# Rotation in four pieces one step apart, and the last unit's value products two ticks behind, in a two-layer decoder trunk on one core

## The reference

```python
def rope(t, positions):
    ...
    t1, t2 = tf[..., :half], tf[..., half:]
    return jnp.concatenate([t1 * cos - t2 * sin, t2 * cos + t1 * sin], axis=-1)

qb_rot = rope(qb, positions)                 # B: queries, 4 tiles
k_sel  = rope(ksb, positions)                # B: selected keys, 1 tile
k_win  = rope(kwb, positions)                # B: window keys, 1 tile
qc = rope(qc, positions)                     # C: queries, 4 tiles
kc = rope(kc, positions)                     # C: keys, 4 tiles
...
    w = prob[:, :, 0] - lam * prob[:, :, 1]              # differential attention
    return jnp.einsum('bhqk,bkhe->bqhe', w, v)
out = rmsnorm(out, subln_g) * (1.0 - lam_init)           # needs all of a head's output
```

## Time and profile before

| | |
|---|---|
| median of 3 runs (lowest to highest) | 1534.54 us (1533.0 to 1534.96) |
| the profiled execution | 1534.6 us |
| its span, first to last instruction | 1532.8 us |
| granted TensorE clock, mean | 0.996 |
| PE busy | 1498.8 us (98%), 7957 matmuls |
| DVE busy | 935.4 us (61%) |
| ACT busy | 634.6 us (41%) |
| POOL busy | 74.4 us (5%) |

### The profile page before, as it was taken

The page is one execution under the profiler, slowest core; times in us unless marked ns, Lnnn a source line. Parts: engine busy times, 40 slices in busy tenths (PEclk is TensorE's granted clock), DMA queues, the critical chain, the costliest instruction groups (busy, mean ns, idle before and its releaser), DMA issues.

```text
span 1532.8 us, 22548 instructions
## 1 busy us (share of the span) xinstructions
PE 1498.8 (98%) x7957; PEld 1205.8 (79%) x7957; DVE 935.4 (61%) x2197; ACT 634.6 (41%) x1499; POOL 74.4 (5%) x80
## 2 busy tenths in 40 slices
PE   8999999999999999999999999999999999999997
PEld 6778777777787777888787887777887887778885
DVE  6866755555556766454576667655555666755544
ACT  6544433334344444343444334334333444434343
POOL 1000000000000010000100000000000000000011
PEclk9999999999999999999999999999999999999998
DMA  7333332222223332332342334222222233233221
GB/s 197 84 83 90 97 77 63 56 69 62 70 63 96 93 80 83 105 105 70 107 108 69 103 83 117 56 57 62 63 63 76 70 96 89 72 101 100 86 86 72
DMA packets 250301, 129.50 MB, mean 84 GB/s; under 512 B 45690, under 2 KB 245972, under 8 KB 250196
## 3 DMA queue, kind: packets, MB, share of 16 engines
q1 hardware_dynamic: 250196, 128.13, 31.4%
HBM read 118.67 MB, written 2.10 MB: 79 GB/s over the span
## 4 chain that ended last, share of the span: by engine, by line
PE 88%; DVE 6%; ACT 3%; issue 2%; DMA 0%; SPq 0%; ACTq 0%; DVEq 0%
PE D L748 24%; PE D L750 22%; PE D L749 22%; PE Ob L936 7%; PE S L895 5%; PE T L914 4%; DVE w_lo L1304 2%; ACT w_hi L1066 1%; PE Mb L952 1%; ACT probs L1182 1%; DVE v_b L1399 1%; PE Mb L862 1%; PE Ob L940 1%; PE Mb L829 1%; DMA acc<-in_x_dram 0%
## 5 line engine op out<-in xcount | busy, mean ns | idle before, releaser
L748 PE MATMUL D<-h_hi,w_hi 128*128 128x512 f32 x1264 | 544.8, 431 | 4.7 <-DVE w_lo L1304 2.3
L750 PE MATMUL D<-h_lo,w_hi 128*128 128x512 f32 x1264 | 496.4, 393 | 0.0
L749 PE MATMUL D<-h_hi,w_lo 128*128 128x512 f32 x1264 | 494.6, 391 | 0.0
L1304 DVE TENSOR_TENSOR w_lo<-raw,w_hi 128x512 fp32r<-128x512 f32 (+2 forms) x504 | 293.9, 622 | 296.3 <-ACT w_hi L1066 296.1
L1066 ACT ACTIVATE w_hi<-raw 128x512 fp32r<-128x512 f32 (+2 forms) x504 | 263.5, 568 | 292.0 <-PE D L750 289.3
L1182 ACT ACTIVATE probs<-probs,nmax 128x128 f32<-128x128 f32 (+3 forms) x256 | 141.9, 555 | 358.7 <-DVE nmax L1554 358.6
L748 PEld LDWEIGHTS D<-h_hi,w_hi 128*128 128x128 f32 x1264 | 238.5, 189 | 65.4 <-issue 20.6
L750 PEld LDWEIGHTS D<-h_lo,w_hi 128*128 128x128 f32 x1264 | 237.3, 188 | 53.2
L749 PEld LDWEIGHTS D<-h_hi,w_lo 128*128 128x128 f32 x1264 | 239.4, 189 | 30.3 <-issue 0.5
L1554 DVE CUSTOM_DVE_ANT_0 probs<-S,maskb 128x128 f32<-128x128 f32 (+3 forms) x256 | 115.0, 486 | 44.6 <-PE S L895 28.7
L546 DVE COPY pT<-T 128x128 f32<-128x128 f32 (+3 forms) x160 | 77.4, 486 | 60.7 <-PE T L914 59.9
(11 more groups left out here) (245 smaller groups left out, 1495.6 us busy)
## 6 DMA issues: line engine op xcount, KB each, us to landing
raw<-in_w_in_dram SPq DMA_DIRECT2D x124, 512.0 KB, 3.9
raw<-in_w_in_dram SPq DMA_DIRECT2D x32, 256.0 KB, 3.8
raw<-in_w_out_dram SPq DMA_DIRECT2D x16, 512.0 KB, 4.1
raw<-in_w_ple_gate_dram SPq DMA_DIRECT2D x16, 512.0 KB, 4.2
rs<-rx SPq DMA_DIRECT2D x80, 64.0 KB, 2.0
raw<-in_cmp_w_k_dram SPq DMA_DIRECT2D x8, 512.0 KB, 3.7
raw<-in_cmp_w_v_dram SPq DMA_DIRECT2D x8, 512.0 KB, 3.8
raw<-in_w_br_a_dram SPq DMA_DIRECT2D x16, 256.0 KB, 2.9
```

The costliest lines, as they stand in the source:

```text
L748: pe.matmul(o, w_hi[:, sl, cs], hi[:, k, :], start=(k == 0), stop=False)
L749: pe.matmul(o, w_lo[:, sl, cs], hi[:, k, :], start=False, stop=False)
L750: ins = pe.matmul(o, w_hi[:, sl, cs], lo[:, k, :], start=False, stop=last)
L1304: TT(w_lo[:, sl, half], raw[:, ring(L, t, RAW), half], f(w_hi[:, sl, half]), ALU.subtract).then_inc(M["dve_lo"], 1)
```

## The change

The rotation becomes four items. "swap" (now 7 steps behind the tile's end instead of 8) holds POOL's sine product and also DVE's cosine product, which leaves the tile's end; "rot" (10 instead of 11) holds only DVE's addition; "high" (11) ACT's rounding; "low" (12) DVE's subtraction. In the last unit, V comes two ticks behind T instead of one, and Y of that unit two ticks behind the last V instead of three.

```diff
             if kind in ROTATED:
-                follow.append([8, ("swap", t)])
-                follow.append([11, ("rot", t)])
+                follow.append([7, ("swap", t)])
+                follow.append([10, ("rot", t)])
+                follow.append([11, ("high", t)])
+                follow.append([12, ("low", t)])
...
-                    vq.append((tick + 1, ti))
+                    vq.append((tick + (2 if u == UNITS - 1 else 1), ti))
...
-                            late.append((tick + (2 if u < UNITS - 1 else 3), ("Y", u)))
+                            late.append((tick + 2, ("Y", u)))
...
-        elif it[0] == "rot":
+        elif it[0] == "low":
             qk_ready.add(tiles[it[1]][:2])
...
-                        elif what == "rot":
+                        elif what == "high":
...
-                            elif kind in ROTATED:
-                                r = rots.after(t)
-                                dve.wait_ge(M["act_evac"], act_evac.after(t))
-                                if r > 1:
-                                    dve.wait_ge(M["qk_s"], r - 1)
-                                TT(rc[:], (qf if kind == "qb" else rx)[:], cosT[:], ALU.mult).then_inc(M["dve_rm"], 1)
...
                         elif what == "rot":
                             t = it[1]
-                            hi_, lo_, u = rot_dst(*tiles[t][:2])
                             r = rots.after(t)
                             dve.wait_ge(M["pool_rot"], r)
                             dve.wait_ge(M["dve_rm"], r)
                             TT(rc[:], rc[:], rb[:], ALU.add).then_inc(M["dve_rs"], 1)
+                        elif what == "swap":
+                            t = it[1]
+                            r = rots.after(t)
+                            dve.wait_ge(M["act_evac"], act_evac.after(t))
+                            if r > 1:
+                                dve.wait_ge(M["qk_s"], r - 1)
+                            TT(rc[:], (qf if tiles[t][0] == "qb" else rx)[:], cosT[:], ALU.mult).then_inc(M["dve_rm"], 1)
+                        elif what == "low":
+                            t = it[1]
+                            hi_, lo_, u = rot_dst(*tiles[t][:2])
+                            r = rots.after(t)
                             dve.wait_ge(M["act_rot"], r)
                             TT(lo_, rc[:], f(hi_), ALU.subtract).then_inc(M["qk_s"], 1)
```

## The result

The changed kernel takes 1536.39 us (median of 22 runs, 1535.73 to 1539.02), the kernel before 1534.83 us (median of 22 runs, 1532.54 to 1535.54). The ratio is 1.0016, with a 95% interval of 1.0009 to 1.0023: slower by 0.16%, some 2.4 us by the ratio (the two medians are 1.56 us apart). The profiled execution's span is 1534.4 us.

A forecast was written before the change was run, and what follows sets the result against it. PE was taken as the bound, busy 1498.8 of 1532.8 us. Losses 1.76 + 0.32 less gain 0.63 gave +1.45 a layer, +2.9 us on 1534.6: 1537.4, said as 1537.2; own range 1536.3 to 1538.3, overall 1533.0 to 1538.9.

The forecast's parts named there:

- the rival in which the chain to Y is no bound: Last unit: N of block 3 comes as soon as PE is done, gain 1.38 a layer, 1536.0 us; chance 0.13.
- Sum ahead of the maxima: At `qb1`, `qb2`, `qc0`: row maxima and PE's value products come later, loss 0.60 + 0.56 + 0.60 = 1.76 us a layer.
- Other rotations at no cost: `qb0`, `qb3`, `ksb` and C's other rotations: DVE idle over a microsecond, no cost, or 0.6 each without that cover.
- Cosine product at "swap", loss 0.32 at `kwb`: At `kwb`: POOL's sine product holds up DVE's cosine product, maxima 1.4 us late, PE 0.32 us later a layer.
- the case without the disturbance: At `kwb`, POOL not holding up the cosine product: sum and `zs` come earlier than before, gain 0.22 us.
- The last unit, gain 0.63: PE's stop for `pT` goes, 1.33 us earlier at Y, but a new 0.70 wait for `y_q`: gain 0.63 a layer.
- VectorE's waiting for ACT at the low part "gone": DVE's 19.8 us of waiting for ACT between sum and low part would be gone, without gain for PE.
- the maxima come later but PE doesn't: Value products behind the delayed maxima: PE not delayed, only the last unit counts, 1533.3 or 1533.9 us; chance 0.15.
- The faster rival: PE's stops at 180.70 and 190.21 (`kwb`) go too, up to 3.5 us a layer, 1527.5 us; chance 0.12.
- the clearly slower one: New stop at Y as long as the old, or POOL's disturbance at several of 14 rotations: 1538.8 to 1540; chance 0.15.

The follow-up runs named there:

- the last block alone: The kernel before with V two ticks behind T only for the very last block of unit 11, and Y two behind it: 1530.97 us, ratio 0.9978.

## Why the prediction was right, and where it was not

The time, the sign and the size came out: 1537.2 was said, 1536.39 measured; the working had +2.9 us, the steps in the table add up to 2.0. The time alone would have proved little. It lies 0.1 us above the lower end of my own range (1536.3 to 1538.3) and nearer to the 1536.0 of the rival in which the chain to Y is no bound. It is the trace that separates the two.

- **Sum ahead of the maxima: right in size, not quite in the path.** Said 0.60, 0.56, 0.60 a layer; measured 0.49 to 0.61, six times. Putting the sum back behind the maxima removes all six. What I had not worked out is that PE pays a part of it already at the transposes, and at `qc0` all of it: the value products there don't move away from the dense step ahead of them, because PE waited for the copy before the change too. Nor was the 0.06 us between copy and value product slack. In the changed kernel, where PE waits, the value product at `qb1` starts 0.05 us behind the copy's end as well.
- **Other rotations at no cost: right but for one.** `ksb` in layer 1 loses 0.13, since the cosine product was moved; at the others nothing over 0.1 is seen.
- **Cosine product at "swap", loss 0.32 at `kwb`: wrong in sign.** The term was to cost 0.32 a layer; the step measured is -0.20 and -0.23. What failed is the time at which the cosine product starts. "By that row the cosine product ends near 186.1 instead of 185.3" puts it at 184.63, where the maxima had started, 0.38 us behind POOL. But the same edit takes the cosine product away from the tile's end, so VectorE reaches `kwb` earlier. The rows before and after:

```profile
180.56 0.68 DVE L1460 TENSOR_TENSOR rc<-rx,cosT 128x512 f32<-128x512 f32 x1
...
184.28 0.29 DVE L1601 TENSOR_TENSOR y_q<-Ob,coef 128x128 f32<-128x128 f32 x1
...
183.69 0.29 DVE L1607 TENSOR_TENSOR y_q<-Ob,coef 128x128 f32<-128x128 f32 x1
```

`y_q` starts 0.59 us earlier. PE's dense products and POOL's sine product there are only 0.29 and 0.30 earlier, which is the offset of the two executions; the other 0.3 us is what VectorE gained. The cosine product then starts 0.21 behind `y_q`, at 183.90, and so 0.05 ahead of POOL. The one that stood was POOL. What I had given for the case without the disturbance, a gain of 0.22, is about what was measured. The mechanism itself holds: with the order of arrival turned round, the loss against the kernel before is 0.28 and 0.25. With the sign right, the sum would have been 1.76 - 0.22 - 0.63 = 0.91 a layer, 1.8 us. The error of 0.5 us a layer is more than the whole difference between 2.9 and 2.0; some 0.1 a layer that the last unit gave less than said goes the other way.

The Trainium skill (SBUF — State Buffer, Who interferes with whom) says that issue order decides who blocks. The two runs agree with it: 0.68 and 1.79 us with VectorE first, 1.82 and 1.29 with POOL first.
- **The last unit, gain 0.63: right.** 0.51 and 0.53 measured; the wait at Y 0.55 where 0.70 was said. The reason given (ACT's `w_hi` behind the square of block 2, behind the `pT` copy) is the order seen in the rows, and it was tested: with the other blocks left where they were, the wait is gone and the gain is 1.37 and 1.42.
- **VectorE's waiting for ACT at the low part "gone": wrong.** It went from 19.8 to 18.1 us. As said beforehand, PE doesn't depend on it, so the sum didn't suffer.
- **The rivals.** That the maxima come later but PE doesn't, and that the chain to Y is no bound, both fell with the first trace. The faster rival needed PE's stop at 180.70 to shrink; it is 1.13 us in the changed kernel too. Of the clearly slower one the disturbance did occur at several of the 14 places, but PE shows no step where VectorE's cosine product was stretched.

## What to carry to other kernels

An operation with slack, moved one place forward on an engine that is late, delays everything the late engine owes: look at what stands between the old place and the new, and at whether the next engine is already waiting for it. When a stop is removed by making work later, move only the piece that was waited for; moving its siblings as well put their follow-up work in front of the next chain, and gave back more than half. Two overlapping products of VectorE and POOL, both with two inputs in SBUF, have two outcomes, and the order of their starts decides. An edit moves both starts, so work out both times anew for the kernel after the edit, and price both orders where they come out within a few tenths of each other.

## What the runs showed of the hardware that was not expected

Hundredths of a microsecond at the start decide whether VectorE stands for over a microsecond or POOL for half of one: VectorE 183.90 and POOL 183.95 gave 0.68 and 1.79 us; 183.91 and 183.90 gave 1.82 and 1.29. In layer 1, VectorE 0.02 us ahead gave 0.68 and 1.82, and 0.03 behind gave 1.79 and 1.28.

In two of the profiled executions TensorE's granted clock fell once, for some microseconds, from its level of 2.4 GHz to that of 1.2 GHz. In the one with the sum a step later (stretch in us, its length; PE, PEld, DVE, ACT, POOL busy, clock, DMA share, GB/s):

```profile
962.00:966.00 4.00, 4.00 (x18) 3.36 (x16) 3.33 (x12) 1.30 (x5) 0.00 (x0) 0.57 0.50 131
```

PE made 18 matmuls in a stretch of 4 us, where the kernel before has 27 at the same place, and the dense products were 1.6 us later behind it. Ahead of the dip PE had waited 0.73 us for `vbd` (every trace of the study has this wait there, with 0.73 to 0.77); why this execution alone lost the clock stays open. In the execution with the last block alone the dip lies at 12 to 20 us (0.75 and 0.82) and costs 0.9. Such a dip is as large as the effects studied here, so single times of one execution are no measure of them, and the steps in the table and the text leave it out. The runs' times go with the clock in the same way. Of the 22 runs of the changed kernel, the five from 1537.9 to 1539.0 us have a mean granted clock of 0.994 or 0.995, and the other 17, from 1535.7 to 1536.5 us, have 0.996 or 0.997.
